# Layer norm behind the depthwise convolution: VectorE adds the two blocks of channels, TensorE sums over one block

## The chip, the cores and the metric

One core of a Trainium2 chip. The number is the time on the device in microseconds, the median of several executions. The engines work side by side and meet at semaphores: TensorE (PE in the profile) multiplies matrices from SBUF into PSUM banks, VectorE (DVE) and ScalarE (ACT) work elementwise, GpSimd (POOL) takes a few operations, SyncE (SP) asks for the transfers of the weights. Each engine works through a list of its own, in order.

## The reference, cut to what matters

Two transformer blocks of two layers each work on 256 positions with 1024 features. In the first block each layer has three mixers: differential attention, pooling, and a convolution over 256 channels with a layer norm behind it. In layer 0 this is computed for the tokens (stream x) and for the context (stream c), in layer 1 for x alone.

```
def layer_norm(x, g, b):
    xf = x.astype(jnp.float32)
    mu = jnp.mean(xf, axis=-1, keepdims=True)
    var = jnp.mean(jnp.square(xf - mu), axis=-1, keepdims=True)
    y = (xf - mu) * lax.rsqrt(var + EPS)
    return (y * g.astype(jnp.float32) + b.astype(jnp.float32)).astype(x.dtype)

def conformer_conv(a, b, dw_w, dw_b, ln_g, ln_b):
    u = a * jax.nn.sigmoid(b)
    y = lax.conv_general_dilated(
        u, dw_w[:, None, :].astype(u.dtype), window_strides=(1,),
        padding=((CONV_PAD, CONV_PAD),), dimension_numbers=('NWC', 'WIO', 'NWC'),
        feature_group_count=CONV_WIDTH)
    y = layer_norm(y + dw_b, ln_g, ln_b)
    return jax.nn.silu(y)
```

The norm is over the 256 channels, so it is called three times: layer 0 for x and for c, layer 1 for x.

## The kernel before

Features lie across the 128 partitions, positions along the free dimension (T = 256). The 256 channels of the convolution are two blocks of 128 partitions, `pc[s][:, 2, :]` and `pc[s][:, 3, :]` for stream s; the rows call them pcx and pcc. A sum over channels is a sum across partitions, and TensorE makes it with a matmul whose weights are a block of ones (a part of the constant `cst`): the result has the sum in every partition. An fp32 matmul is two records in the trace.

A plan is written once (`plan_program`): each `step` has a name and its data, and every engine walks through the same list of steps and emits its own part of each (`walk`). So the order of the steps is the order in every engine's list, and a wait holds up all that stands behind it on that engine. `ev` gives a step's result a semaphore and a value; `wait_ge` waits for it; `banks` and `tmps` hand out PSUM banks and SBUF buffers of 128x512.

The order around the norm is written out by hand, in `IN_FIRST` for layer 0 and `IN_SECOND` for layer 1. Each string is a list of portions that are put between two steps of the attention: `c` and `x` are `finish_conv`, the first step of the norm for that stream (`conv1`), `N` is `conv_norm`, the second step (`conv2`) for all streams that wait for it, `A` the third (`conv3`, ScalarE's silu), `m` a modulation piece (TensorE's matmuls of `raw` with `csil`, which then free a weight buffer), `t` four taps of the convolution, `s` and `h` the splitting of a weight piece into its high and low parts, `G`, `K` and `P` a piece of the input projection. In layer 0 the strings that matter are `"m x t"`, `"c m m"` and `"S m h N s m"`, where `N` works on x and then on c; in layer 1 they are `"K S m"`, `"x"`, `"N h m h A m"`.

The attention between them goes step by step: VectorE takes the maximum of the scores (`TENSOR_REDUCE`), ScalarE the exponential, VectorE scales the two maps and subtracts them (the last of these is `SCALAR_TENSOR_TENSOR e<-e,st,e`), TensorE transposes them, multiplies with v (`aT,v`), sums the squares for the head's norm (`tmp,cst`) and makes the next scores (`k,q1x`). ScalarE's root is a logarithm and an exponential.

The norm of a stream before the change:

- `conv1`: TensorE waits for the taps and adds up two matmuls, one for each block, in bank m. VectorE subtracts m/256 from both blocks (two operations). ScalarE squares both blocks into the buffer `sq`, one operation over 512 columns.
- `conv2`: TensorE waits for the squares and adds up two matmuls in bank v. ScalarE makes the root `rs`. VectorE multiplies both blocks with it, one operation.
- `conv3`: ScalarE's silu with gain and shift, on a table of its own, loaded before and given back after it.

The weights come through three buffers `raw`; a piece's transfer is asked for when the buffer's last reader is done.

## Time and profile before

| what | us |
|---|---|
| median of 3 executions | 1646.68 (1646.48 to 1648.18) |
| the profiled execution | 1644.55 |
| its span in the trace | 1642.8 |
| TensorE busy | 1589.0 |
| VectorE busy | 1129.8 |
| ScalarE busy | 919.0 |

The times of the rows are microseconds from the start of the span, in the profiled execution. A record of VectorE or ScalarE can begin a little before the one ahead of it has ended. The rows of one engine in a timeline are merged where they are alike: x4 with 1.13 us are four records, two fp32 matmuls. The mean of TensorE's granted clock is 0.995 over the span; 1.00 is its upper level, 0.50 its lower.

### The profile page before, as it was taken

What the parts mean: (1) busy time and instruction counts of PE and PEld (TensorE: products, weight loads), DVE (VectorE), ACT (ScalarE), POOL (GpSimd) and SP (SyncE); (2) the same over time, 40 slices, a digit from 0 to 9 for tenths busy, and PEclk for the clock granted to TensorE, in tenths of its full rate; (3) what the DMA queues carried; (4) which work ended last, traced back from release to release, by engine and by line L of the source; (5) the groups of instructions that cost most, each with busy time, mean ns of one, the idle gap of its engine ahead of it and who ended that gap; (6) DMA issues with size and microseconds to landing.
All of it is one profiled execution on the core that took longest, in us unless ns stands there. A gap on an engine that the chain in (4) does not pass through costs nothing. (4 is left out here: it accounts for less than half of the span.)

```text
span 1642.8 us, 31046 instructions
## 1 busy us (share of the span) xinstructions
PE 1589.0 (97%) x12874; PEld 1463.2 (89%) x12874; DVE 1129.8 (69%) x1763; ACT 919.0 (56%) x1459; POOL 127.2 (8%) x106
## 2 busy tenths in 40 slices
PE   6999999999999999999999999999999999999999
PEld 3987478999999999966899999878999998799999
DVE  2799677645566655897765556778887567788873
ACT  3444756545365444647554446767666467676662
POOL 0230000112001100300011000000101000001110
PEclk9999999999999999999999999999999999999999
DMA  9443666656546555435566653323555533245553
GB/s 395 160 152 131 258 236 227 235 216 240 192 167 221 205 188 201 155 125 207 195 228 237 220 184 119 118 78 130 207 191 202 204 112 116 77 137 200 207 193 118
DMA packets 46172, 303.36 MB, mean 185 GB/s; under 512 B 5072, under 2 KB 7376, under 8 KB 12752
## 3 DMA queue, kind: packets, MB, share of 16 engines
q1 hardware_dynamic: 45312, 299.78, 50.7%
q8 instruction: 102, 1.67, 0.4%
q0 software_dynamic: 288, 0.92, 0.1%
q10 hardware_dynamic: 432, 0.68, 0.1%
q14 instruction: 38, 0.31, 0.1%
HBM read 298.22 MB, written 3.15 MB: 183 GB/s over the span
## 5 line engine op out<-in xcount | busy, mean ns | idle before, releaser
L2002 DVE TENSOR_TENSOR wl<-raw,wh 128x1040 fp32r<-128x1040 f32 (+1 forms) x472 | 576.4, 1260 | 295.8 <-ACT wh L1759 229.9
L1759 ACT ACTIVATE wh<-raw 128x1040 fp32r<-128x1040 f32 (+1 forms) x472 | 466.5, 1031 | 195.5 <-PE bank L1552 109.3
L1547 PE MATMUL bank<-hx_hi,wh 128*128 128x256 f32 x1856 | 519.6, 280 | 6.0 <-ACT hx_hi L1759 3.8
L1552 PE MATMUL bank<-hx_lo,wh 128*128 128x256 f32 x1856 | 516.2, 278 | 0.0
L1550 PE MATMUL bank<-hx_hi,wl 128*128 128x256 f32 x1856 | 514.7, 277 | 0.3 <-DVE wl L2002 0.2
L1547 PEld LDWEIGHTS bank<-hx_hi,wh 128*128 128x128 f32 x1856 | 349.0, 188 | 10.8 <-issue 9.8
L1550 PEld LDWEIGHTS bank<-hx_hi,wl 128*128 128x128 f32 x1856 | 349.1, 188 | 2.8 <-issue 1.7
L1552 PEld LDWEIGHTS bank<-hx_lo,wh 128*128 128x128 f32 x1856 | 348.8, 188 | 1.0 <-DVE hx_lo L1995 0.4
L1550 PE MATMUL bank<-hid_hi,wl 128*128 128x256 f32 x912 | 252.2, 277 | 1.4 <-DVE wl L2002 1.4
L1547 PE MATMUL bank<-hid_hi,wh 128*128 128x256 f32 x912 | 252.5, 277 | 0.3 <-ACT wh L1759 0.2
L1552 PE MATMUL bank<-hid_lo,wh 128*128 128x256 f32 x912 | 251.9, 276 | 0.0
L1547 PE MATMUL bank<-hc_hi,wh 128*128 128x256 f32 x784 | 223.1, 285 | 3.2 <-issue 3.2
L1552 PE MATMUL bank<-hc_lo,wh 128*128 128x256 f32 x784 | 218.4, 279 | 1.2 <-DVE hc_lo L2139 1.2
L1550 PE MATMUL bank<-hc_hi,wl 128*128 128x256 f32 x784 | 218.1, 278 | 0.0
L1550 PEld LDWEIGHTS bank<-hid_hi,wl 128*128 128x128 f32 x912 | 171.2, 188 | 1.8 <-DVE wl L2002 1.8
L1547 PEld LDWEIGHTS bank<-hid_hi,wh 128*128 128x128 f32 x912 | 171.2, 188 | 0.7 <-ACT wh L1759 0.7
L1552 PEld LDWEIGHTS bank<-hid_lo,wh 128*128 128x128 f32 x912 | 171.2, 188 | 0.0
L1547 PEld LDWEIGHTS bank<-hc_hi,wh 128*128 128x128 f32 x784 | 148.1, 189 | 14.2 <-issue 11.4
L1552 PEld LDWEIGHTS bank<-hc_lo,wh 128*128 128x128 f32 x784 | 148.0, 189 | 1.6 <-DVE hc_lo L2139 1.4
L1550 PEld LDWEIGHTS bank<-hc_hi,wl 128*128 128x128 f32 x784 | 148.2, 189 | 0.9 <-issue 0.7
L1759 ACT ACTIVATE tmp<-bank 128x512 f32<-128x512 f32 (+4 forms) x102 | 57.0, 562 | 122.5 <-PE bank L1552 100.8
L1759 ACT ACTIVATE tmp<-bank,vec 128x256 f32<-128x256 f32 (+3 forms) x180 | 100.0, 582 | 40.8 <-PE bank L1575 34.7
(218 smaller groups left out, 1891.5 us busy)
## 6 DMA issues: line engine op xcount, KB each, us to landing
raw<-in_wts SPq DMA_DIRECT2D x208, 1032.0 KB, 4.9
raw<-in_wts SPq DMA_DIRECT2D x50, 1024.0 KB, 6.6
raw<-in_wts SPq DMA_DIRECT2D x20, 776.0 KB, 4.3
raw<-in_wts SPq DMA_DIRECT2D x4, 584.0 KB, 4.4
tscr<-tmp SPq DMA_DIRECT2D x4, 512.0 KB, 7.4
bias<-tscr SPq DMA_DIRECT2D x4, 512.0 KB, 6.0
raw<-in_wts SPq DMA_DIRECT2D x2, 648.0 KB, 4.0
xTc<-in_ctxT SPq DMA_DIRECT2D x1, 1024.0 KB, 10.6
```

The source lines that it names most:

```text
L1547: pe.matmul(out, block(f, M.wh, w0 + k, ncols, c, m), x_hi, start=first and k == 0 and o == 0, stop=False, skip_group_check=True)
L1550: pe.matmul(out, block(f, M.wl, w0 + k, ncols, c, m), x_hi, start=False, stop=False, skip_group_check=True)
L1552: ins = pe.matmul(out, block(f, M.wh, w0 + k, ncols, c, m), x_lo, start=False, stop=last and k == nk - 1, skip_group_check=True)
L1759: return act.activation(out, in_, func, bias=bias, scale=scale)
L2002: tt(M.wl[k][:, cols], M.raw[r][:, cols], M.wh[k][:, cols].bitcast(F32), ALU.subtract).then_inc(*on.inc(lo))
```

## The change

In `conv1` VectorE first adds the two blocks into the first half of `sq`, and TensorE has one matmul over this sum. In `conv2` VectorE adds the two halves of the squares in place, and TensorE has one matmul over that. Both additions have an event of their own (t_p), and TensorE waits for it in place of the taps or the squares. The buffer `sq` is taken where it was before, but is written earlier, by VectorE. Everything else is as it was.

```diff
--- before.py
+++ after.py
@@ -752,16 +752,16 @@
 
     def conv_post(l, s):
         m = banks.get()
-        t, t_d = ev("mm"), [ev("cdev"), ev("cdev")]
+        t_p, t, t_d = ev("cdev"), ev("mm"), [ev("cdev"), ev("cdev")]
         sq = tmps.get()
         a = ev("csq")
-        step("conv1", s=s, m=m, m_free=m.free, ready=conv_tok[s], sq=sq, sq_free=sq.free, t=t, t_d=t_d, a=a)
+        step("conv1", s=s, m=m, m_free=m.free, ready=conv_tok[s], sq=sq, sq_free=sq.free, t_p=t_p, t=t, t_d=t_d, a=a)
         banks.give(m, t_d[1])
 
         def two():
             v, rs = banks.get(), tmps.get()
-            t2, t_ln, t_rs, t_n = ev("mm"), ev("ln"), ev("rs"), ev("cdev")
-            step("conv2", s=s, v=v, v_free=v.free, sq=sq, a=a, rs=rs, rs_free=rs.free, t=t2, t_ln=t_ln,
+            t_p2, t2, t_ln, t_rs, t_n = ev("cdev"), ev("mm"), ev("ln"), ev("rs"), ev("cdev")
+            step("conv2", s=s, v=v, v_free=v.free, sq=sq, a=a, t_p=t_p2, rs=rs, rs_free=rs.free, t=t2, t_ln=t_ln,
                  t_rs=t_rs, t_n=t_n)
             tmps.give(sq, t2)
             banks.give(v, t_ln)
@@ -1623,17 +1623,13 @@
             ins = mm(b.t[:, j * T:j * T + T], M.poolw[:, 2 * l + j, :], M.pc[s][:, j, :], j == 0, True)
         ins.then_inc(*on.inc(t))
 
-    def conv1(s, m, m_free, ready, t, **_):
-        on.wait_ge(ready, m_free)
-        for j in range(2):
-            ins = mm(m.t[:, 0:T], M.ones, M.pc[s][:, 2 + j, :], j == 0, j == 1)
-        ins.then_inc(*on.inc(t))
-
-    def conv2(v, v_free, sq, a, t, **_):
-        on.wait_ge(a, v_free)
-        for j in range(2):
-            ins = mm(v.t[:, 0:T], M.ones, sq.t[:, j * T:j * T + T], j == 0, j == 1)
-        ins.then_inc(*on.inc(t))
+    def conv1(m, m_free, sq, t_p, t, **_):
+        on.wait_ge(t_p, m_free)
+        mm(m.t[:, 0:T], M.ones, sq.t[:, 0:T], True, True).then_inc(*on.inc(t))
+
+    def conv2(v, v_free, sq, t_p, t, **_):
+        on.wait_ge(t_p, v_free)
+        mm(v.t[:, 0:T], M.ones, sq.t[:, 0:T], True, True).then_inc(*on.inc(t))
 
     def sc1(s, h, qt, L, sc, free, ready, ts, **_):
         on.wait_ge(ready)
@@ -2093,15 +2089,19 @@
         else:
             stt(y, src, wk, y, ALU.mult, ALU.add).then_inc(*on.inc(t))
 
-    def conv1(s, m, ready, t, t_d, **_):
-        on.wait_ge(t, ready)
+    def conv1(s, m, ready, sq, sq_free, t_p, t, t_d, **_):
+        on.wait_ge(ready, sq_free)
+        tt(sq.t[:, 0:T], M.pc[s][:, 2, :], M.pc[s][:, 3, :], ALU.add).then_inc(*on.inc(t_p))
+        on.wait_ge(t)
         for j in range(2):
             y = M.pc[s][:, 2 + j, :]
             stt(y, m.t[:, 0:T], -1.0 / 256, y, ALU.mult, ALU.add).then_inc(*on.inc(t_d[j]))
 
-    def conv2(s, rs, a, t_rs, t_n, **_):
+    def conv2(s, sq, rs, a, t_p, t_rs, t_n, **_):
         y = M.pc[s][:, 2:4, :]
-        on.wait_ge(t_rs, a)
+        on.wait_ge(a)
+        tt(sq.t[:, 0:T], sq.t[:, 0:T], sq.t[:, T:2 * T], ALU.add).then_inc(*on.inc(t_p))
+        on.wait_ge(t_rs)
         tt(y, y, rs.t[:, 0:T].unsqueeze(1).to_broadcast([P, 2, T]), ALU.mult).then_inc(*on.inc(t_n))
 
     def exp1(L, sc, ts_=None, d=None, d_free=None, t_m=None, **k):
```

The places where this changes the lists of the engines are three norms with two steps each; two places of layer 0 stand here. e is a map of the attention, st its statistics, tmp_81 and tmp_85 the buffers `sq` of c and x, raw and csil the modulation. The line numbers of helpers move by four, since the changed functions are shorter.

VectorE, first step of stream c in layer 0, before:

```order
L1991 TENSOR_SCALAR st_69<-st_69,nlam 128x1 [waits s_awt]
L1991 TENSOR_SCALAR e_0_95<-e_0_95,st_69 128x256 [waits s_awt]
L1995 SCALAR_TENSOR_TENSOR e_0_94<-e_0_94,st_69,e_0_95 128x256 [waits s_awt]
L1995 SCALAR_TENSOR_TENSOR pcc<-bank,pcc 128x256 [waits s_mm]
L1995 SCALAR_TENSOR_TENSOR pcc<-bank,pcc 128x256
L2111 TENSOR_REDUCE st_60<-bank 128x1 x2
L1991 TENSOR_SCALAR st_60<-st_60 128x2 [waits s_amax]
```

and after:

```order
L1987 TENSOR_SCALAR st_69<-st_69,nlam 128x1 [waits s_awt]
L1987 TENSOR_SCALAR e_0_95<-e_0_95,st_69 128x256 [waits s_awt]
L1991 SCALAR_TENSOR_TENSOR e_0_94<-e_0_94,st_69,e_0_95 128x256 [waits s_awt]
L2094 TENSOR_TENSOR tmp_81<-pcc 128x256
L1991 SCALAR_TENSOR_TENSOR pcc<-bank,pcc 128x256 [waits s_mm]
L1991 SCALAR_TENSOR_TENSOR pcc<-bank,pcc 128x256
L2111 TENSOR_REDUCE st_60<-bank 128x1 x2
L1987 TENSOR_SCALAR st_60<-st_60 128x2 [waits s_amax]
```

The addition stands behind the attention's last scaling and in front of the subtraction, which waits for TensorE in both.

TensorE at the same place, before:

```order
L1575 MATMUL bank<-k_90,q1x 128x512 [waits s_aexp] x2
L1575 MATMUL bank<-pcc,cst 128x256 [waits s_ln]
L1575 MATMUL bank<-pcc,cst 128x256
L1575 MATMUL bank<-raw_56,csil 32x512 [waits s_raw1]
L1575 MATMUL bank<-raw_56,csil 32x512 x3
L1575 MATMUL bank<-raw_57,csil 32x512 [waits s_raw2]
L1575 MATMUL bank<-raw_57,csil 32x512 x3
```

and after:

```order
L1575 MATMUL bank<-k_90,q1x 128x512 [waits s_aexp] x2
L1575 MATMUL bank<-tmp_81,cst 128x256 [waits s_ln,s_cdev]
L1575 MATMUL bank<-raw_56,csil 32x512 [waits s_raw1]
L1575 MATMUL bank<-raw_56,csil 32x512 x3
L1575 MATMUL bank<-raw_57,csil 32x512 [waits s_raw2]
L1575 MATMUL bank<-raw_57,csil 32x512 x3
```

Where two matmuls read pcc with no wait for VectorE, one reads tmp_81 and waits for an event of VectorE (s_cdev); the modulation matmuls stand behind it.

VectorE, second steps of x and c in layer 0, before:

```order
L1991 TENSOR_SCALAR e_0_95<-e_0_95,st_60 128x512 [waits s_awt]
L1995 SCALAR_TENSOR_TENSOR e_0_94<-e_0_94,st_60,e_0_95 128x512 [waits s_awt]
L2105 TENSOR_TENSOR pcx<-pcx,tmp_84 128x512 [waits s_csq,s_rs]
L2105 TENSOR_TENSOR pcc<-pcc,tmp_83 128x512 [waits s_csq,s_rs]
L2111 TENSOR_REDUCE st_63<-bank 128x1 [waits s_mm] x2
L1991 TENSOR_SCALAR st_63<-st_63 128x2 [waits s_amax]
```

and after:

```order
L1987 TENSOR_SCALAR e_0_95<-e_0_95,st_60 128x512 [waits s_awt]
L1991 SCALAR_TENSOR_TENSOR e_0_94<-e_0_94,st_60,e_0_95 128x512 [waits s_awt]
L2103 TENSOR_TENSOR tmp_85<-tmp_85 128x256 [waits s_csq]
L2105 TENSOR_TENSOR pcx<-pcx,tmp_84 128x512 [waits s_rs]
L2103 TENSOR_TENSOR tmp_81<-tmp_81 128x256 [waits s_csq]
L2105 TENSOR_TENSOR pcc<-pcc,tmp_83 128x512 [waits s_rs]
L2111 TENSOR_REDUCE st_63<-bank 128x1 [waits s_mm] x2
L1987 TENSOR_SCALAR st_63<-st_63 128x2 [waits s_amax]
```

The addition of c stands behind the product of x, which waits for the root (s_rs).

TensorE at the same place, before:

```order
L1575 MATMUL bank<-k_90,q1x 128x512 [waits s_aexp] x2
L1575 MATMUL bank<-raw_56,csil 32x512 [waits s_raw1]
L1575 MATMUL bank<-raw_56,csil 32x512 x3
L1575 MATMUL bank<-tmp_85,cst 128x256 [waits s_ln,s_csq]
L1575 MATMUL bank<-tmp_85,cst 128x256
L1575 MATMUL bank<-tmp_81,cst 128x256 [waits s_subln,s_csq]
L1575 MATMUL bank<-tmp_81,cst 128x256
L1575 MATMUL bank<-raw_57,csil 32x512 [waits s_raw2]
```

and after:

```order
L1575 MATMUL bank<-k_90,q1x 128x512 [waits s_aexp] x2
L1575 MATMUL bank<-raw_56,csil 32x512 [waits s_raw1]
L1575 MATMUL bank<-raw_56,csil 32x512 x3
L1575 MATMUL bank<-tmp_85,cst 128x256 [waits s_ln,s_cdev]
L1575 MATMUL bank<-tmp_81,cst 128x256 [waits s_subln,s_cdev]
L1575 MATMUL bank<-raw_57,csil 32x512 [waits s_raw2]
```

The four matmuls in a row have become two, each with a wait for VectorE where it was one for ScalarE's squares (s_csq).

## Rows read from the trace of the kernel before

**Rows 1.** The page, first part: busy us, share of the span, instructions.
```profile
PE 1589.0 (97%) x12874; PEld 1463.2 (89%) x12874; DVE 1129.8 (69%) x1763; ACT 919.0 (56%) x1459; POOL 127.2 (8%) x106
```

**Rows 2.** Timeline: start, us, engine, line, out<-in, idle before; layer 0, x, first step.
```profile
169.57 0.48 DVE L1995 SCALAR_TENSOR_TENSOR e<-e,st,e 128x256 f32<-128x256 f32 x1
...
170.96 1.13 PE L1575 MATMUL bank<-pcx,cst 128*128 128x256 f32 x4
...
172.13 0.76 DVE L1995 SCALAR_TENSOR_TENSOR pcx<-bank,pcx 128x256 f32<-128x256 f32 x2 [2.07 <-PE bank L1575]
```

**Rows 3.** Timeline, layer 0, stream c, first step.
```profile
176.97 1.13 PE L1575 MATMUL bank<-pcc,cst 128*128 128x256 f32 x4
...
178.00 0.48 DVE L1995 SCALAR_TENSOR_TENSOR e<-e,st,e 128x256 f32<-128x256 f32 x1
178.03 1.92 PE L1575 MATMUL bank<-raw,csil 128*32 128x512 f32 x16
```

**Rows 4.** Timeline, layer 0: one attention norm, from its matmul to its product.
```profile
182.23 0.70 PE L1575 MATMUL bank<-tmp,cst 128*128 128x256 f32 x2
...
182.86 1.06 PE L1575 MATMUL bank<-raw,csil 128*32 128x512 f32 x8
182.96 0.47 ACT L1759 ACTIVATE tmp<-bank,vec 128x256 f32<-128x256 f32 x1
...
183.92 0.48 DVE L1995 SCALAR_TENSOR_TENSOR q1c<-bank,sub,tmp 128x256 f32<-128x256 f32 x1 [2.14 <-ACT tmp L1759]
```

**Rows 5.** Timeline, layer 0, second steps of both streams and what follows.
```profile
186.28 1.99 PE L1575 MATMUL bank<-tmp,cst 128*128 128x256 f32 x8
...
186.68 0.75 DVE L1995 SCALAR_TENSOR_TENSOR e<-e,st,e 128x512 f32<-128x512 f32 x1
...
188.20 1.06 PE L1575 MATMUL bank<-raw,csil 128*32 128x512 f32 x8
...
189.26 0.69 DVE L2105 TENSOR_TENSOR pcc<-pcc,tmp 128x512 f32<-128x512 f32 x1 [0.17 <-ACT tmp L1759]
...
196.32 0.16 PEld L1575 LDWEIGHTS bank<-raw,csil 128*32 128x32 f32 x8 [0.76 <-DMA raw<-in_wts]
...
199.08 1.13 PE L1575 MATMUL bank<-aT,v 128*128 128x256 f32 x4 [1.70 <-ACT aT L1759]
```

**Rows 6.** Timeline, layer 1, stream x, both steps.
```profile
737.10 1.13 PE L1575 MATMUL bank<-pcx,cst 128*128 128x256 f32 x4
...
739.04 0.75 DVE L1995 SCALAR_TENSOR_TENSOR e<-e,st,e 128x512 f32<-128x512 f32 x1
...
739.70 0.75 DVE L1995 SCALAR_TENSOR_TENSOR pcx<-bank,pcx 128x256 f32<-128x256 f32 x2
...
741.49 1.13 PE L1575 MATMUL bank<-tmp,cst 128*128 128x256 f32 x4
...
742.73 0.75 DVE L1995 SCALAR_TENSOR_TENSOR e<-e,st,e 128x512 f32<-128x512 f32 x1
...
743.31 0.47 ACT L1759 ACTIVATE tmp<-bank,vec 128x256 f32<-128x256 f32 x1
...
750.30 0.70 PE L1575 MATMUL bank<-tmp,cst 128*128 128x256 f32 x2 [2.40 <-ACT tmp L1759]
```

**Rows 7.** One line's instructions: count, duration ns min/median/max, first and last start.
```profile
L2040 DVE TENSOR_TENSOR tmp<-tmp x10: 424/425/426, 15.3 to 1456.2; 128x256 f32<-128x256 f32 x10
```

**Rows 8.** Stretches: from:to, length, busy PE, PEld, DVE, ACT, POOL, granted clock, DMA.
```profile
206.00:208.00 2.00, 0.00 (x0) 0.00 (x0) 1.67 (x2) 2.00 (x3) 0.00 (x0) 1.00 0.93 388
208.00:210.00 2.00, 0.58 (x3) 0.40 (x3) 1.84 (x2) 0.89 (x2) 0.00 (x0) 0.93 1.03 435
210.00:212.00 2.00, 2.00 (x10) 2.00 (x11) 1.60 (x2) 2.00 (x3) 0.00 (x0) 0.50 0.97 393
212.00:214.00 2.00, 2.00 (x14) 2.00 (x14) 2.00 (x3) 1.14 (x2) 0.00 (x0) 0.72 1.02 324
...
748.00:750.00 2.00, 0.00 (x0) 0.00 (x0) 1.86 (x7) 1.97 (x4) 0.00 (x0) 1.00 1.01 426
```

## Prediction

> **What bounds the kernel now.** I read the page's busy shares first: TensorE is busy 97% of the span [rows 1], VectorE much less. So a matmul taken away can pay, and an operation added to VectorE can be free, but only if nobody waits for it. Four places decide that: the two steps of the layer norm for stream x and stream c in layer 0, and for stream x in layer 1. I went through the timeline around each of them. In all of them the reader should compare two starts: when TensorE comes to the norm's matmuls, and when VectorE, which works in the order of its own list, comes to the norm's operation. For the first step of stream c TensorE is there at 176.97, while VectorE is still in the attention's scaling until 178.48 [rows 3]. For the second steps TensorE is there at 186.28 and VectorE is busy until 187.43 [rows 5]. In layer 1 it is 737.10 against 739.79, and later 741.49 against 743.48 [rows 6]. Only for the first step of stream x in layer 0 is VectorE early: it has finished at 170.05 and TensorE comes at 170.96 [rows 2]. Before the change this order costs nothing, since the matmuls read what was finished long ago (the taps and ScalarE's squares).
>
> **What the change removes.** Six matmuls of 128x256, one in each step of three norms. Each shows as two records, so x2 in a row of the timeline is one matmul. One alone, with the next work behind it, holds TensorE from 182.23 to 182.86, 0.63 us [rows 4]; four in a row hold it from 186.28 to 188.20, 1.92 us [rows 5]. So each further one costs (1.92 - 0.63)/3 = 0.43 us, and six are worth 2.6 us if TensorE never waits.
>
> **What it adds.** Six additions of 128x256 on VectorE. The trace has the same operation in the fold of the other norm: 0.425 us [rows 7], taken as 0.43 us here. Apart from the matmuls the order on TensorE stays. But each norm matmul now waits for VectorE's addition, and behind it in TensorE's list stand the modulation matmuls, the next attention values, transposes and scores; none of them needs the norm, all of them wait. VectorE too now stands still between its addition and the answer. I go by the trace's own clock of events and start each addition at the end of the record before it.
>
> *Stream x, first step, layer 0.* The addition runs from 170.05 to 170.48, before TensorE is there at 170.96 [rows 2]: covered. TensorE gains 0.43 us, and so does everything behind it.
>
> *Stream c, first step.* VectorE ends its scaling at 178.48 - 0.43 = 178.05 [rows 3]; the addition ends at 178.48; the matmul starts there and the next work 0.63 us later, at 179.11. Before, it started at 178.03 [rows 3]. The loss so far is 1.1 us, the two matmuls saved included.
>
> *The second steps in layer 0.* Both stand in a row on VectorE: addition x, wait for x's root, product x, addition c, wait, product c. VectorE ends its scaling at 187.43 + 1.08 = 188.51 [rows 5], the addition for x ends at 188.94. From the start of a matmul to the product that waits for ScalarE's logarithm and exponential it takes 183.92 - 182.23 = 1.69 us [rows 4]: 190.63. The product takes 0.69 [rows 5], so 191.32; the addition for c ends at 191.75; the matmul starts there and the modulation matmul behind it at 192.38, where it was 188.20 [rows 5]. **Layer 0 loses 4.2 us**, all savings counted. ScalarE and VectorE are as late there as TensorE is, since c's product, too, is 4.1 to 4.2 us later. After this ScalarE is the one that is waited for: TensorE stands still before 199.08 for its copy [rows 5], and that copy is late by as much. I see nothing fixed in time behind which the loss could vanish.
>
> *Layer 1, stream x.* VectorE ends its scaling at 739.79 [rows 6]; the addition ends at 740.22 and the matmul, which ran at 737.10, starts. The subtraction came 172.13 - 170.96 = 1.17 us after the start of two matmuls [rows 2], so 0.74 after one: 740.96 against the 739.70 of before [rows 6], 1.26 late. The scaling that follows ends at 743.48 + 1.26 = 744.74, the second addition at 745.17. The matmul starts there; ScalarE's logarithm follows 182.96 - 182.23 = 0.73 later [rows 4], at 745.90 where it was 743.31 [rows 6]. From there ScalarE works without a pause through two table loads, and TensorE, held at 750.30 by ScalarE [rows 6], is 2.6 us late. TensorE itself loses more (its modulation matmuls come 3.2 us later), but it had 2.4 us of idle time there [rows 6].
>
> The sum of the waits is 4.2 + 2.6 = **6.8 us**. Its lower bound, with everything saved and nothing waited for, is -2.6 us. It is too high by up to 0.4 us where an addition starts a little before the record before it ends.
>
> How long an addition takes is also where a page speaks. The row says 0.425 us [rows 7]. The Trainium skill, "VectorE: DVE Perf Modes", in the section on the 1x mode, gives a two-input fp32 operation one result per cycle at 0.96 GHz, an estimate of 0.27 us for 256 columns. With it five exposed additions would be 0.16 us shorter each, and the sum 6.0 instead of 6.8. The row includes what lies around the stream of elements and decides.
>
> **The clock.** TensorE's granted clock falls from its 2.4 to its 1.2 GHz level after thin stretches: it stands idle from 206 to 208, and the clock's mean is 0.93, 0.50 and 0.72 in the three slices of 2 us behind that [rows 8]. That is 0.28 + 2 + 1.12 = 3.4 us at half speed, worth 1.7 us of matmuls. The changed kernel makes such stretches: between 187.4 and 191.75 in layer 0 TensorE would do a single norm matmul, and in layer 1 it would stand still for 3 us before 740.2 and again for 2.6 before 745.2. A fall in layer 0 meets dense matmuls on which the rest waits; I take half of the 1.7, 0.9 us. In layer 1 it meets mostly work that has slack behind ScalarE, and stretches only two short norm matmuls; I take 0.3. Against it: 2.4 us of idle time before 750.3 brought no fall (clock 1.00) [rows 8]. The Trainium skill, "Trainium Architecture — The Big Picture", in the section on what this means for kernel authors, says that TensorE runs at 1.2 or 2.4 GHz depending on its recent activity; by that, a further fall is likelier than none, and the trace's fall agrees.
>
> **The forecast.** 6.8 + 1.2 = 8.0 us. The profiled execution took 1644.55 us (span 1642.8), 2.1 less than the median of 1646.68; both move by the same 8 us, to about 1652.6 for such a run and 1654.7 for the median.
>
> **The rivals.**
> - *The waits, but no further fall of the clock.* 6.8 us, 1653.5. For it: the two gaps in layer 0 are 1.4 and about 2.2 us, neither longer than the 2.4 us that brought nothing [rows 8].
> - *More than the replay shows.* Both falls cost their full 1.7 us, or the norms of attention, late by now, open a gap that I took as closed: 6.8 + 3.4 = 10.2, 1656.9, and up to 1660.
> - *The weights' transfers swallow layer 0's part.* Before 196.32 the weight load waited 0.76 us for a piece [rows 5]. If transfers set the pace there, TensorE catches up while they run on, and only layer 1's 2.6 us stay: 1649.3, within 0.2%, so not slower. It decides if the pieces land at fixed times; against it, only three buffers exist, each is asked for again only when TensorE has read it, and the largest wait of this kind is 0.76 us.
> - *The waits are hidden.* If all additions came before TensorE needs them, 2.6 us are gained: 1644.1. The point at which it would decide is the order of the two starts, and in five of the six places VectorE is late, by 1.2 to 2.7 us (186.28 against 187.43 is the smallest [rows 5], 737.10 against 739.79 the largest [rows 6]).
>
> **How the numbers follow.** Forecast with the clock 0.45; waits alone 0.25; more than that 0.15; swallowed in layer 0 0.12; hidden 0.03. What a measurement of this kernel can tell is about 0.2%, 3.3 us, so the sides end at 1643.4 and 1650.0. Slower: 0.45 + 0.25 + 0.15, and 0.02 from the fourth case where it swallows less, 0.87. Same: 0.11. Faster: 0.02. The range runs from 1650.5 to 1658: it leaves out the last two cases and the upper third of the third.
>
> **What the profile of the changed kernel would show.** TensorE's six sums of one block each; the one of stream c held near 178.5 by an addition on VectorE; the two of the second step no longer in a row but about 2.8 us apart, the second 5.5 us later than the pair of before began; in layer 1 the matmul near 740.2 and not at 737.1, and the one near 745.2. TensorE's idle time between 176 and 206 should grow by some 5 us, and slices at 0.50 should appear near 190 to 195 and near 741. I would be wrong if VectorE reached its additions before TensorE did, if the modulation matmul that was at 188.20 started before 191, or if TensorE's restart after 205 came at its old time: the first would be an error of the order, the last one of the slack.

## The result

| | before | after |
|---|---|---|
| median, us | 1646.68 (1646.18 to 1648.18, 5 executions) | 1659.79 (1654.57 to 1661.89, 5 executions) |
| profiled execution, us | 1644.55 | 1659.79 |
| its span, us | 1642.8 | 1658.0 |
| mean granted clock of TensorE | 0.995 | 0.986 |

The changed kernel is slower: ratio 1.007, 95% interval 1.0051 to 1.0089. That is 13.1 us by the medians, where 8.0 were forecast, and above the range's end of 1658.

The page of the changed kernel, its first lines; the one of before stands in [rows 1]:

```profile
span 1658.0 us, 31025 instructions
## 1 busy us (share of the span) xinstructions
PE 1596.0 (96%) x12862; PEld 1464.8 (88%) x12862; DVE 1131.3 (68%) x1769; ACT 918.6 (55%) x1459; POOL 127.0 (8%) x106
```

TensorE has twelve records fewer (six matmuls) and is busy for 7.0 us *longer*. Taking work away can't do that; a lower clock can. The other 8.2 us between the two spans are idle time.

The waits of TensorE in the changed kernel (releaser and line waited for: us in total, times, longest us). Neither line had a counterpart before:

```profile
PE bank L1575 <- DVE tmp L2103: 4.9, 3, 2.1
PE bank L1575 <- DVE tmp L2094: 4.8, 2, 2.9
```

L2094 is the addition ahead of the mean's sum, L2103 the one ahead of the variance's. Five of the six sums wait for it, 9.7 us together. The sixth, for x in layer 0, is early, as the prediction had it.

The timeline of TensorE in layer 0 of the changed kernel, from c's mean to the modulation matmul behind both variances (start and length in us, line, operation, idle time before it and its releaser), and then VectorE's two additions that the sums at 179.84 and 191.89 wait for:

```profile
176.88 1.13 PE L1575 MATMUL bank<-k,q1x 64*128 64x512 f32 x4
179.84 1.16 PE L1575 MATMUL bank<-tmp,cst 128*128 128x256 f32 x2 [1.83 <-DVE tmp L2094]
180.92 3.10 PE L1575 MATMUL bank<-raw,csil 128*32 128x512 f32 x16
...
191.89 0.70 PE L1575 MATMUL bank<-tmp,cst 128*128 128x256 f32 x2 [1.48 <-DVE tmp L2103]
194.67 1.22 PE L1575 MATMUL bank<-tmp,cst 128*128 128x256 f32 x2 [2.07 <-DVE tmp L2103]
195.82 1.94 PE L1575 MATMUL bank<-raw,csil 128*32 128x512 f32 x8
```

```profile
179.36 0.42 DVE L2094 TENSOR_TENSOR tmp<-pcc 128x256 f32<-128x256 f32 x1
...
191.42 0.42 DVE L2103 TENSOR_TENSOR tmp<-tmp 128x256 f32<-128x256 f32 x1
```

Compare the lengths of the same work. One sum takes 0.70 us in the row at 191.89 and 1.22 at 194.67. Eight modulation records take 1.94 us at 195.82; before, the same eight took 1.06 [rows 5]. The second values are TensorE at its lower clock. The stretches show it (columns: length, then busy time of PE, PEld, DVE, ACT and POOL, the granted clock, share and rate of the DMA queues):

```profile
176.00:180.00 4.00, 2.17 (x15) 0.67 (x8) 2.78 (x9) 2.20 (x8) 0.00 (x0) 0.99 0.71 240
180.00:184.00 4.00, 4.00 (x19) 0.91 (x19) 2.83 (x9) 0.63 (x1) 0.00 (x0) 0.58 0.29 86
184.00:188.00 4.00, 4.00 (x25) 1.75 (x22) 0.43 (x2) 2.80 (x8) 0.00 (x0) 1.00 0.87 320
188.00:192.00 4.00, 2.52 (x15) 0.69 (x15) 3.70 (x9) 1.83 (x5) 0.00 (x0) 1.00 1.00 360
192.00:196.00 4.00, 1.93 (x8) 0.87 (x12) 1.03 (x2) 0.96 (x3) 0.00 (x0) 0.70 0.91 350
196.00:200.00 4.00, 4.00 (x15) 1.87 (x11) 2.98 (x8) 1.62 (x4) 0.00 (x0) 0.50 0.32 86
```

TensorE was busy for 2.17 of 4 us ahead of the first fall, and for 2.52 and 1.93 of 4 around the start of the second. Layer 1 has the longest one; 749 to 761 is at the lower level throughout, and the sums are slow there too:

```profile
748.00:752.00 4.00, 1.06 (x4) 0.73 (x3) 2.82 (x8) 1.45 (x4) 0.00 (x0) 0.74 0.58 239
752.00:756.00 4.00, 3.10 (x9) 1.16 (x7) 3.58 (x10) 2.56 (x6) 0.00 (x0) 0.50 0.01 4
756.00:760.00 4.00, 3.54 (x14) 1.09 (x18) 1.39 (x4) 2.25 (x4) 0.00 (x0) 0.50 0.00 0
```

```profile
751.02 1.22 PE L1575 MATMUL bank<-tmp,cst 128*128 128x256 f32 x2 [2.94 <-DVE tmp L2094]
...
756.46 1.22 PE L1575 MATMUL bank<-tmp,cst 128*128 128x256 f32 x2 [1.36 <-DVE tmp L2103]
```

Added up over slices of 1 us, the time at the lower level around the norms and behind them is: before, 3.4 us at 209 to 214, 3.4 at 725 to 729 and 3.4 at 803 to 808. After, 3.4 at 179 to 184, 6.8 at 193 to 201, 6.8 at 217 to 225, 3.4 at 736 to 740, 10.2 at 749 to 761 and 3.4 at 818 to 822. So there are 24 us more of it.

Where the 15.2 us between the two spans come in, by the start of the same instruction in each trace (us). The last column is a kernel explained below, with TensorE kept at work in the waits:

| place | before | after | with the waits filled |
|---|---|---|---|
| end of the start-up (a subtraction of VectorE ahead of the norm) | 166.29 | 167.69 | 167.69 |
| TensorE's restart for layer 0's output projection | 208.22 | 218.84 | 213.63 |
| rope (the rotation by position) in layer 1 on VectorE | 721.84 | 732.67 | 728.40 |
| TensorE's start of layer 1's feed-forward part | 802.92 | 818.24 | 812.02 |
| end of the span | 1642.8 | 1658.0 | 1651.1 |

After against before, that is 1.4 us in the start-up, which the change doesn't touch, 9.2 in layer 0's norm and what follows it, 0.2 up to layer 1, 4.5 in layer 1, and -0.1 behind it. The start-up's share is no effect of the change: its end lay anywhere from 166.29 to 168.12 in the profiles of this study, all of which have the same program up to there.

Each column is one execution, and that of the kernel before is 2.1 us under its median. So the traces say where the time goes, and the medians how much it is.

### The profile page after: what moved, and what is told of

The parts are those of the page before. It is cut to its first block and busy times, and to the rows that moved or that the text cites. A ratio compares the mean times of both kernels' runs of the same rounds, so it can differ in the third digit from the quotient of the medians.

```text
span 1658.0 us, 31025 instructions
## 1 busy us (share of the span) xinstructions
PE 1596.0 (96%) x12862; PEld 1464.8 (88%) x12862; DVE 1131.3 (68%) x1769; ACT 918.6 (55%) x1459; POOL 127.0 (8%) x106
## 5 line engine op out<-in xcount | busy, mean ns | idle before, releaser
L1547 PEld LDWEIGHTS bank<-hc_hi,wh 128*128 128x128 f32 x784 | 148.4, 189 | 15.2 <-issue 11.7
```

What stands on the lines that cost most here:

```text
L1547: pe.matmul(out, block(f, M.wh, w0 + k, ncols, c, m), x_hi, start=first and k == 0 and o == 0, stop=False, skip_group_check=True)
```

## The experiments

Each kernel was timed next to the kernel before, which in these rounds had a median of 1646.8 to 1646.9. Times are medians, the ratio is to the kernel before, with its 95% interval. Where nothing else is said, a diff is against the changed kernel.

### One step at a time

The mean's sums from VectorE, the variance's as before:

```diff
-    def conv2(v, v_free, sq, t_p, t, **_):
-        on.wait_ge(t_p, v_free)
-        mm(v.t[:, 0:T], M.ones, sq.t[:, 0:T], True, True).then_inc(*on.inc(t))
+    def conv2(v, v_free, sq, a, t, **_):
+        on.wait_ge(a, v_free)
+        for j in range(2):
+            ins = mm(v.t[:, 0:T], M.ones, sq.t[:, j * T:j * T + T], j == 0, j == 1)
+        ins.then_inc(*on.inc(t))
```

> Only the first steps of the norm (the mean) take the sum of the two blocks from VectorE; the second steps (the variance) are the old ones, with two matmuls. By the theory that the time is TensorE's waits for VectorE plus half-clock time that follows such waits: the trace of the changed kernel shows 1.83 us of wait ahead of c's first sum in layer 0 and 2.94 us ahead of x's in layer 1, next to 2.0 us for the three matmuls removed where they stood in view, so a net of +3 us of waits, and one or two stretches of 3.4 us at half clock in addition, 1.7 us each: 1650 to 1653. By the rival that only the waits count: 1649.7, and no new half-clock stretch beside this kernel's layer norm. By the rival that most of the loss is in the second steps: within 1 us of 1646.7.

Measured: 1651.39 us, 1.003 (1.0019 to 1.0041), in the range of the theory. TensorE waits 4.8 us for the two additions, and the lower clock shows at 180 to 184 and for 6.8 us at 743 to 751.

The other way round, `conv1` as before and `conv2` changed:

> Only the second steps (the variance) take the sum from VectorE; the mean's sums are the old pairs of matmuls. By the theory of waits plus clock: 1.48 and 2.07 us of wait ahead of the two variance sums of layer 0 and 1.36 us in layer 1, less 1.3 us for three matmuls, and half-clock stretches behind them (two of 3.4 us in layer 0, one or two in layer 1, 1.7 us each): 1651 to 1656. By the rival that only waits count: 1650.3. The two single changes together should make up the +13.1 us of the whole if each place costs by itself; by the clock they need not, since one half-clock stretch makes the next wait longer or shorter.

Measured: 1654.1 us, 1.0046 (1.0033 to 1.0058), in the range of the theory. The three waits are 5.9 us, and 191 to 198 is at the lower clock. The two steps cost 4.6 and 7.3 us, 12.0 together, of the 13.1 of the whole. Both steps cost. The rival that the loss sits in the second steps is out, and so is the one that only the waits count (1649.7 and 1650.3): both traces have low clock right behind the waits.

### What the additions cost by themselves

TensorE's pairs of matmuls and its waits as before. VectorE makes the six additions all the same, and no sum reads them (cut: TensorE's part of `conv2` goes back in the same way as that of `conv1`):

```diff
-        on.wait_ge(t_p, m_free)
-        mm(m.t[:, 0:T], M.ones, sq.t[:, 0:T], True, True).then_inc(*on.inc(t))
+        on.wait_ge(ready, m_free)
+        for j in range(2):
+            ins = mm(m.t[:, 0:T], M.ones, M.pc[s][:, 2 + j, :], j == 0, j == 1)
+        ins.then_inc(*on.inc(t))
...
-        tt(sq.t[:, 0:T], sq.t[:, 0:T], sq.t[:, T:2 * T], ALU.add).then_inc(*on.inc(t_p))
+        tt(rs.t[:, T:2 * T], sq.t[:, 0:T], sq.t[:, T:2 * T], ALU.add).then_inc(*on.inc(t_p))
```

> The old pairs of matmuls and the old waits of TensorE, but VectorE makes the six additions too, at the places in its order where the change has them; no sum reads them. This prices the additions alone. Theory that TensorE's waits for the additions are the cost: each addition delays VectorE's next work by 0.43 us, of which only those ahead of work that TensorE waits for show, 1646.7 to 1648.5. Rival that VectorE's extra work by itself makes the loss (its waits ahead of the squares, its later subtractions and products): 1654 or more.

Measured: 1648.0 us, 1.0005 (0.9997 to 1.0014). VectorE's extra work alone can't be told from nothing; the interval leaves room for 2.3 us at most, of 13.1. In its trace layer 0 takes as long as before from the end of the start-up to the restart (41.96 and 41.93 us). So the loss needs TensorE to wait for the additions.

### Is the excess the clock?

The changed kernel, but TensorE works on matmuls that nobody reads while it would wait for the addition. The numbers of matmuls are 0, 3, 6 ahead of the mean's sums and 3, 5, 5 ahead of the variance's (cut: `conv2` calls `fill` in the same way):

```diff
+    fills = {"conv1": [0, 3, 6], "conv2": [3, 5, 5]}
+
+    def fill(name, bank, free):
+        on.wait_ge(free)
+        for _ in range(fills[name].pop(0)):
+            mm(bank.t[:, 0:T], M.ones, M.cst[:, 0:T], True, True)
+
     def conv1(m, m_free, sq, t_p, t, **_):
-        on.wait_ge(t_p, m_free)
+        fill("conv1", m, m_free)
+        on.wait_ge(t_p)
         mm(m.t[:, 0:T], M.ones, sq.t[:, 0:T], True, True).then_inc(*on.inc(t))
```

> The changed kernel with matmuls (ones times a constant block, 128x256) put into TensorE's waits for the additions: none, three and six ahead of the three mean sums and three, five and five ahead of the three variance sums, 0.43 us each at full clock. They write the bank that the sum then overwrites, so nothing that is computed changes; they keep TensorE at work while it would have waited. Theory that the excess over the replayed waits is half-clock time brought on by the idle stretches: no new half-clock stretch around the norm, and 1653 to 1655, about 5 us below the changed kernel's 1659.8. Rival that the additions themselves and their waits are simply longer than was worked out: 1659 to 1661, with the waits in the trace replaced by the matmuls. Rival that half clock comes from elsewhere: the stretches remain and the time is 1660 or more.

Measured: 1652.85 us, 1.004 (1.0026 to 1.0054). *More* work on TensorE makes the changed kernel 6.9 us faster, a little more than the theory's 1653 to 1655. Both rivals (1659 and more) are out. From 37 us to the restart at 213.63, and from 222 us to the end of layer 1, this trace has no slice below the upper clock. Its layer 1, where the changed kernel was at 0.50 for 12 us (busy time and clock as above):

```profile
744.00:748.00 4.00, 2.16 (x13) 1.44 (x13) 3.07 (x9) 1.45 (x4) 0.00 (x0) 1.00 0.14 56
748.00:752.00 4.00, 3.63 (x16) 2.21 (x14) 3.46 (x9) 2.56 (x6) 0.00 (x0) 1.00 0.00 0
752.00:756.00 4.00, 4.00 (x27) 2.03 (x26) 2.32 (x3) 3.56 (x5) 0.00 (x0) 1.00 0.36 102
```

This kernel is also close to the replay of the prediction: the waits, with the clock held. Rows of layer 0, the filling matmuls being those with only cst behind the arrow, and among them VectorE's addition for the variance of x:

```profile
177.90 1.56 PE L1575 MATMUL bank<-cst 128*128 128x256 f32 x6
179.80 0.70 PE L1575 MATMUL bank<-tmp,cst 128*128 128x256 f32 x2 [0.33 <-DVE tmp L2103]
180.43 1.92 PE L1575 MATMUL bank<-raw,csil 128*32 128x512 f32 x16
...
189.74 0.42 DVE L2112 TENSOR_TENSOR tmp<-tmp 128x256 f32<-128x256 f32 x1
...
192.99 0.70 PE L1575 MATMUL bank<-tmp,cst 128*128 128x256 f32 x2
193.62 1.06 PE L1575 MATMUL bank<-raw,csil 128*32 128x512 f32 x8
```

and of VectorE and TensorE in layer 1 (the last scaling, the subtraction, and TensorE held by ScalarE):

```profile
745.59 0.75 DVE L2000 SCALAR_TENSOR_TENSOR e<-e,st,e 128x512 f32<-128x512 f32 x1
...
747.47 0.76 DVE L2000 SCALAR_TENSOR_TENSOR pcx<-bank,pcx 128x256 f32<-128x256 f32 x2 [0.79 <-PE bank L1575]
```

```profile
759.37 0.70 PE L1575 MATMUL bank<-tmp,cst 128*128 128x256 f32 x2 [1.74 <-ACT tmp L1764]
```

They are read against the prediction below.

### Layer 1 alone

Layer 0 as before, layer 1 as changed (two pairs of matmuls become additions and single matmuls):

> Only layer 1's two sums are changed, as in the change; layer 0 keeps the four pairs of matmuls. The sum on record gave layer 1 waits of +2.6 us and 0.3 us of clock: 1649.6. By the trace of the changed kernel, with 10.2 us at half clock from 749 on where there were 3.4 us at 803 to 808 before: +2.6 and 3 to 5 us of clock, 1652 to 1654. If layer 1 costs nothing because the next stage waits for weights anyway: 1646.7.

Measured: 1650.92 us, 1.0024 (1.0016 to 1.0033). 4.2 us, between the sum on record (1649.6) and the estimate from the changed kernel's trace (1652 to 1654), so neither hit. In this execution TensorE came to the sum sooner, having had no low clock at 725, and waited longer:

```profile
742.01 1.22 PE L1601 MATMUL bank<-tmp,cst 128*128 128x256 f32 x2 [4.63 <-DVE tmp L2132]
747.44 0.70 PE L1601 MATMUL bank<-tmp,cst 128*128 128x256 f32 x2 [1.67 <-DVE tmp L2136]
```

From rope to the feed-forward part this trace takes 85.54 us, the changed kernel's 85.57 and the one before 81.08: the same loss with a longer wait. So TensorE's wait is not the price: what counts is VectorE's chain of taps, softmax and additions, and TensorE waits for it from whenever it arrives.

### The additions moved to where VectorE is early

Both mean additions of layer 0 ahead of x's subtraction, both variance additions ahead of the attention's reductions, layer 1's mean addition behind the last tap; layer 1's variance keeps its two matmuls. Each addition is a step of its own, and the order of the steps becomes:

```diff
-IN_FIRST = ("m G", "", "G m", "m G", "G", "G h", "m x t", "m", "c m m", "m h", "S m h N s m", "A m m", "m",
+IN_FIRST = ("m G", "", "G m", "m G", "G", "G h", "m X C x t", "m", "c m m", "V m h", "S m h N s m", "A m m", "m",
...
-IN_SECOND = ("K P s s", "m P", "K S m", "x", "N h m h A m", "Z P s s", "m h m", "", "t O m", "", "m O", "")
+IN_SECOND = ("K P s s", "m P", "K S C m", "x", "N h m h A m", "Z P s s", "m h m", "", "t O m", "", "m O", "")
```

Here x and c are the norm's first steps, X and C the additions for them, V both variance additions.

> Five of the six sums over one block, with VectorE's additions moved to where VectorE has idle time or is ahead of TensorE: both mean additions of layer 0 ahead of x's subtraction, where VectorE waited 1.30 us for TensorE; both variance additions of layer 0 ahead of the reductions that precede the sums; the mean addition of layer 1 right behind the last tap. The variance sum of layer 1 keeps its two matmuls. Theory that only the place of the additions made the loss: no wait of TensorE for the additions, no new half-clock stretch around the norm, five matmuls of 0.43 us gone, 1646.7 - 2.1 = 1644.6. Rival that VectorE's 0.43 us pieces come back as later waits: 1646.7 to 1648. Rival that the change costs wherever it is placed: 1650 or more.

Measured: 1650.22 us, 1.0023 (1.0014 to 1.0033). 3.5 us slower than before, so the theory (1644.6) and the rival of later waits (up to 1648) fell. The number is that of the third case, that the change costs wherever it is placed (1650 or more); the kernels at the end of the next section show that it doesn't have to. Most of the loss against the changed kernel is gone, but the matmuls removed bring nothing. In layer 0 the order is right now: TensorE waits for no addition, and reaches the modulation matmul at 186.81, 1.8 us sooner than before if one counts from the end of the start-up. But then it waits for ScalarE:

```profile
198.98 3.52 PE L1602 MATMUL bank<-aT,v 128*128 128x256 f32 x8 [2.79 <-ACT aT L1794]
```

In [rows 5] this wait was 1.70 us and ended at 199.08. ScalarE's rows show why it doesn't end sooner, those of this kernel and then those of the kernel before:

```profile
197.04 1.28 ACT L1785 ACT_TABLE_LOAD   x1
198.33 0.60 ACT L1794 ACTIVATE aT<-bank 128x512 f32<-128x512 f32 x1
```

```profile
197.14 1.28 ACT L1750 ACT_TABLE_LOAD   x1
198.43 0.60 ACT L1759 ACTIVATE aT<-bank 128x512 f32<-128x512 f32 x1
```

The copy aT stands behind ScalarE's exponentials, two silus and their table loads. These hang on VectorE's softmax work. TensorE's gain had brought VectorE 0.9 us forward there (its operation on `q1c` begins 16.7 us behind the end of the start-up, 17.6 us in the kernel before, at 183.92 [rows 4]), and the two additions took nearly all of it back. At 198.98 TensorE is 0.5 us ahead by the same count, not 1.8. The rest turned into waiting, the clock fell behind it, and at its restart, at 209.80, TensorE is 1.2 us late. In layer 1 the addition was not early enough here: TensorE came sooner than in the trace of before, which had a fall at 725 to 729, and waited for it:

```profile
739.63 0.70 PE L1602 MATMUL bank<-tmp,cst 128*128 128x256 f32 x2 [1.78 <-DVE tmp L2133]
```

Two more kernels take the layers apart.

> Layer 0's four sums over one block with all four additions early (as in the run with five early additions); layer 1 keeps its two pairs of matmuls. In that run TensorE reached the projections behind the variance sums 1.8 us earlier, measured from the end of the start-up, and then waited 2.79 us instead of 1.70 us for a block that ScalarE writes behind two table loads, so the layer's end did not move. Theory that the removed matmuls are swallowed by that wait: 1646.7, and up to 1648.5 where the longer wait brings one more half-clock stretch. Rival that the removed matmuls are worth their 1.7 us once the additions are early: 1645.0.

Measured: 1648.64 us, 1.0008 (0.9999 to 1.0017). Four matmuls fewer, no wait for an addition, and still no gain; it even lies just past the upper end of the theory (1648.5). Its stretches show the new fall at 199 to 203, and a longer one behind the restart (6.8 us, where the profile of before has 3.4; that one differs between traces of other kernels too):

```profile
196.00:200.00 4.00, 1.32 (x8) 0.91 (x5) 2.87 (x7) 3.97 (x8) 0.00 (x0) 0.95 1.00 416
200.00:204.00 4.00, 4.00 (x14) 2.37 (x12) 1.61 (x4) 1.57 (x5) 0.00 (x0) 0.63 0.44 184
```

> Only the mean sum of layer 1 is changed, with its addition right behind the last tap; everything else is the kernel before. Theory that VectorE sets the pace there (its softmax work ends at 739.04 and TensorE waits 1.62 us for it), so that an addition ahead of it costs its 0.43 us and the removed matmul is worth nothing, plus up to one half-clock stretch: 1647.1 to 1648.8. Rival that the removed matmul counts: 1646.3. Rival that the sum is late at any place: 1649 or more.

Measured: 1648.16 us, 1.0008 (0.9999 to 1.0017), in the range of the theory, though the interval just touches no change. In this execution, which had a fall at 727 to 732, the sum itself has no wait, and the transposes behind it wait longer for VectorE than the 1.62 us of the kernel before:

```profile
739.52 0.70 PE L1602 MATMUL bank<-tmp,cst 128*128 128x256 f32 x2
742.56 0.66 PE L1683 MATMUL bank<-cst,e 128*128 128x128 f32 x4 [2.34 <-DVE e L2030]
```

The removed matmul and the addition together became 0.7 us of extra idle time. The two layers (+1.8 and +1.3 us against the kernel before of the same rounds) make up 3.1 of the 3.5 us, though neither of the two is clear of the noise by itself.

### Can the clock be held in the kernel before?

The kernel before, with seven and four filling matmuls in two of its own waits (cut: the lines that hand the number to the step; the diff is against the kernel before):

```diff
-    def gemm(f, nk, ncols, tiles, a, a_toks, k0, first, last, free, t_half, w0, t, **_):
+    def gemm(f, nk, ncols, tiles, a, a_toks, k0, first, last, free, t_half, w0, t, fill=0, **_):
+        if fill:
+            on.wait_ge(free[0])
+        for _ in range(fill):
+            mm(tiles[0][3].t[:, 0:T], M.ones, M.cst[:, 0:T], True, True)
```

> The kernel before (all sums over two blocks by two matmuls, no additions), with matmuls that nobody reads put into two of TensorE's own old waits: seven of 128x256 ahead of the output projection of layer 0 (wait 3.16 us before 208.22) and four ahead of the first matrix product of the feed-forward part of layer 1 (wait 2.12 us before 802.92). They write banks that are then overwritten. Theory that idle time brings the clock down: the half-clock stretches 209-214 and 803-808 go, 1.7 us each, 1643.3. Rival that the clock falls for another reason: stretches remain, 1646.7 or slightly more. Rival that the half clock there is hidden behind weight transfers: stretches gone, 1646.7.

Measured: 1644.28 us, 0.9988 (0.9979 to 0.9997). Its rows and the stretches, behind the restart of layer 0 and at the start of layer 1's feed-forward part:

```profile
205.87 3.29 PE L1612 MATMUL bank<-cst 128*128 128x256 f32 x14
209.14 0.36 PE L1584 MATMUL bank<-hc_hi,wh 128*128 128x256 f32 x1
```

```profile
208.00:212.00 4.00, 2.84 (x18) 2.20 (x17) 3.41 (x4) 2.86 (x4) 0.00 (x0) 1.00 1.01 425
212.00:216.00 4.00, 4.00 (x37) 4.00 (x37) 3.96 (x4) 2.06 (x3) 0.00 (x0) 1.00 0.84 279
800.00:804.00 4.00, 3.77 (x16) 3.06 (x17) 1.49 (x8) 1.52 (x3) 0.00 (x0) 1.00 0.56 233
804.00:808.00 4.00, 3.56 (x24) 2.96 (x23) 3.82 (x10) 2.44 (x5) 0.00 (x0) 1.00 0.00 0
```

The same stretches were at 0.71 and 0.86, 0.95 and 0.62 before:

```profile
208.00:212.00 4.00, 2.58 (x12) 2.40 (x13) 3.44 (x4) 2.89 (x4) 0.00 (x0) 0.71 1.00 414
212.00:216.00 4.00, 4.00 (x32) 4.00 (x32) 3.05 (x3) 1.14 (x2) 0.00 (x0) 0.86 0.88 313
...
800.00:804.00 4.00, 1.88 (x9) 1.28 (x8) 2.02 (x5) 2.03 (x5) 0.00 (x0) 0.95 0.09 37
804.00:808.00 4.00, 4.00 (x25) 4.00 (x24) 4.00 (x11) 2.59 (x6) 0.00 (x0) 0.62 0.17 49
```

Both falls are gone, as expected, and 2.5 us of the 3.4 came. The gain is one of the medians; the profiled execution took 1645.71 us and has a fall at 741 to 745 instead of the one at 725 to 729. That the idle stretch makes the fall shows in all traces together: the ten kernels whose wait at the restart of layer 0 is not filled have a fall behind it, of 3.4 or 6.8 us, and the four with it filled (this one and the three below) have none.

Then the filling matmuls with the early additions of the kernel with five of them:

> The early additions and the filling matmuls together. If the two gains are independent, 1646.7 - 2.1 - 3.4 = 1641.2; if one of them gives nothing, 1643 to 1645; if the filling matmuls delay the work behind them, 1646 or more.

Measured: 1647.34 us, 1.0001 (0.9992 to 1.001). The filling takes 2.9 us off the 1650.22, but the early additions keep their cost: it is 3.1 us over the same filling without them, above the 1641.2 and the 1643 to 1645 of the first two cases. The number is that of the third case (1646 or more), but not its reason, since the same filling alone gave a gain. The wait for ScalarE at 199 was not filled here, and the trace has a fall behind it, at 200 to 205. And with two more waits filled, once with layer 0's four early additions and once without additions:

> Layer 0 with the four early additions, and matmuls that nobody reads in four of TensorE's waits (four ahead of the attention product that waits for ScalarE at 199, seven ahead of the output projection at 208, four ahead of the norm's sum at 750, four ahead of the feed-forward part at 803). Theory that the removed matmuls are swallowed and the clock stays up: 1643 to 1644.3, the same as the kernel with filling matmuls alone. Rival that with the clock held up the removed matmuls do count: 1641.5. Rival that filling matmuls delay what is behind them: 1646 or more.

> The kernel before with the same filling matmuls in four waits, no additions, all sums by two matmuls. Two of the four places gave 1644.3 for 1646.8. Theory: each further place at which TensorE is kept at work saves half-clock time: 1643. If the two places had already removed what the clock costs there: 1644.3. If the new ones stand in the way of the sums: 1646.

Measured: 1643.94 us, 0.9982 (0.9974 to 0.9991), and 1645.26 us, 0.9989 (0.998 to 0.9998). The first is the fastest kernel of the study, and its mean clock is 0.998 in the profiled execution. It matches the theory that the removed matmuls are swallowed (1643 to 1644.3). The second missed its 1643: the two further places gave nothing over the 1644.28. The two kernels have the same program from layer 1 on, so layer 0 has to be read by itself. From the end of the start-up to the restart for the output projection (us, one trace each):

| kernel | end of the start-up | restart | between them | at the lower clock in between |
|---|---|---|---|---|
| before | 166.29 | 208.22 | 41.93 | 0 |
| four waits filled, no additions | 167.86 | 209.82 | 41.96 | 0 |
| four early additions | 166.60 | 209.72 | 43.12 | 3.4 |
| four early additions, four waits filled | 166.95 | 208.47 | 41.52 | 0 |

With the clock held, the four early additions bring 0.4 us of the 1.7 that the removed matmuls were worth; without, they cost 1.2 us. The difference, 1.6 us, is what the one new fall at 199 to 203 costs. So what the early additions cost in layer 0 is the clock, and with the clock held most of the gain is still swallowed by the wait for ScalarE. The rest of the 1.3 us between the two medians need not be the additions': in these traces layer 1 takes 81.12 us with them and 82.80 without, from rope to the feed-forward part, and the second has a fall at 738 to 746 where the first has none.

## Why the prediction was right and wrong

**Direction and mechanism: right.** The order of the two starts decided: five additions are late for TensorE, one is early. The rivals that ended at 1653.5 or below are out: the interval around the measured time begins at 1655.1.

**The waits, 6.8 us: right.** The kernel with the waits filled is the nearest test of this term. It is 6.1 us over the kernel before, and its steps fall where the replay put them. In layer 0 this trace's start-up ended 1.40 us later than before (167.69 against 166.29); with that added to the forecast:

| step | forecast + 1.40 | measured |
|---|---|---|
| work behind c's mean sum | 180.51 | 180.43 |
| x's product | 192.03 | 191.90 |
| c's variance sum | 193.15 | 192.99 |
| modulation matmul behind it | 193.78 | 193.62 |

The product at 191.90 is VectorE's `pcx<-pcx,tmp`. Up to the restart behind layer 0, 4.0 us were lost, where 4.2 were forecast; neither trace has low clock in this stretch. In layer 1, measured from the end of VectorE's scaling (739.79 in the working, 746.34 here): the subtraction 1.17 forecast and 1.13 measured; TensorE held by ScalarE's work until 13.1 forecast (750.30 - 739.79 + 2.6) and 13.03 measured. From rope to the feed-forward part the loss is 2.5 us against 2.6. The trace of before has a fall in this stretch, at 725 to 729, and the filled one none; it seems to have cost nothing there, since the kernel with early additions and four waits filled has none either and takes the same 81.1 us. That the losses pass on undiminished, because ScalarE and its table loads are late by as much, held too.

**The length of an addition: right.** 0.42 us in all six rows. The prediction set beside it an estimate of 0.27 us, from a page that gives the rate of such an operation. The same page of the Trainium skill, "VectorE: DVE Perf Modes", has in its section on the TRN2 errata a fixed part of 151 cycles for an fp32 addition of two tensors, at 0.96 GHz; for 256 columns that is an estimate of 0.42 us, and the trace agrees. The estimate of 0.27 us had left the fixed part out.

**The clock, 1.2 us: the step that failed.** Between the kernel with the waits filled and the changed one there are 6.9 us, with the same additions and order. By the sum, 13.1 - 6.8, it is 6.3. Either way the term was taken at a fifth of its size. Three choices went into it:

- *How many falls.* One in layer 0 was counted. There were two (179 to 184, 193 to 201), the second twice as long as the one in [rows 8]. Layer 1 had 10.2 us that were not there before.
- *What a fall hits.* Half of its cost was taken to be hidden in layer 0 and five sixths in layer 1, since ScalarE has the say there. The changed kernel and the filled one left the start-up at the same 167.69, so their times can be set side by side. VectorE's addition for the variance of x comes at 191.42 and at 189.74: the fall at 179 to 184, 3.4 us long, arrives there with its full 1.7 us. At the restart the two are 5.2 us apart (218.84 and 213.63), for 10.2 us at the lower clock, of which half, 5.1 us, is what matmuls lose. In layer 0 nothing was hidden. In layer 1 most of it was, from rope to the feed-forward part 2.0 us were paid (85.6 and 83.6) for 13.6 us at the lower clock, but 0.3 had been taken. One way in which a fall reaches the other engines is the sum on which they wait: for c in layer 0 and for x in layer 1, VectorE's wait between addition and product is 2.27 us in the changed kernel, 1.74 and 1.75 with the clock held.
- *The row that spoke against it.* 2.4 us of idle time before 750.3 without a fall [rows 8] was used for the rival without a fall. In the changed kernel a wait of 1.83 us was followed by one. In these traces the length of one wait doesn't tell whether a fall comes; 2.4 us without one were no cover.

This is the first half of the case that the prediction called "more than the replay shows" (0.15, up to 1660), and more of it: two falls at their full cost were 3.4 us there, and 6.3 to 6.9 were measured. The attention norms that it named besides were not needed.

The changed kernel has 34 us at the lower clock in these places, the filled one 6.8 (behind its restart). 27 us of it cost 6.9 us, 0.25 us for each on average: 0.5 in layer 0, 0.14 in layer 1 (what the two traces differ by in the stretches behind these, -0.9 and +0.7 us, nearly cancels).

**The rival of the weights' transfers: wrong in its place, right in kind.** Nothing swallowed the loss. But in the kernels with early additions something did swallow the *gain*: the wait for ScalarE at 199. The prediction had taken 2.6 us as what six matmuls are worth "if TensorE never waits"; the four of layer 0 brought 0.4 us of their 1.7 with the clock held, and 1.2 us of loss without, when no addition was late. TensorE's 97% of busy time [rows 1] did not mean that a matmul removed in this stretch pays.

**The signs that were named** came out as follows. The variance sums were 2.8 us apart (191.89 and 194.67), as forecast, but the second came 7.0 us later than the pair of before, counted from the end of the start-up, and not 5.5; with the waits filled it is 5.3. c's sum came at 179.84; that is the forecast of 178.5 and 1.4 of start-up. The modulation matmul was at 195.82 and not at its old time. In layer 1 the mean's sum came 18.35 us behind rope (751.02 and 732.67), where 18.38 was forecast (740.22 and 721.84). TensorE's idle time between 176 and 206 grew by 2.7 us (2.6 to 5.4), not by 5, since slow matmuls filled part of this window; up to the restart it grew by 6.2 (5.0 to 11.2). Slices at 0.50 appeared at 194 to 200 and, later than said, from 750 on.

The clock's two levels and that they follow activity is what the Trainium skill says in "Trainium Architecture — The Big Picture", section on what this means for kernel authors; the changed kernel agrees, since work that nobody reads kept its mean clock at 0.994 where it was 0.986.

## What to carry to other kernels

Before moving a sum from TensorE to a slower engine, compare when each engine arrives at it: an addition of 0.42 us cost up to 3 us of waiting, since it stood behind that engine's other work. Price every new idle stretch of TensorE twice, once as waiting and once as the low clock behind it; here the second was as large as the first, and in layer 0 it was paid in full. A wait can be filled with matmuls that nobody reads, but each place has to be measured: two filled places brought 2.5 us, two more brought nothing. And the share of busy time doesn't say that a matmul is worth its length: ask what ends the next wait behind it.

## What was new about the hardware

- Idle time of TensorE is dearer than it looks, and filling it with matmuls that nobody reads pays: 6.9 us in the changed kernel, 2.5 us in the kernel before, for 22 and 11 matmuls of 128x256.
- A fall can come behind waits that are each short: the one at 179 to 184 stood behind a longest wait of 1.83 us, while 2.4 us of idle time before 750.3 had brought none in the kernel before. The fall at 199 to 203 with early additions stood behind a wait of 2.7 us and took 1.6 us.
- The lower clock comes partly at fixed places. Behind the restart of layer 0 each of the ten traces without filling there has it, but for 3.4 us in three and for 6.8 in seven; the falls near 725 and 740 stand in some traces and not in others. Whether this makes the spread between executions of one kernel (1645.4 to 1650.3 us in 33 of the kernel before) isn't shown: the slowest of them has a mean clock of 0.994, one of 1645.55 us has 0.992.
